# Feed-forward units with the hi and lo halves of the input side by side, and the linear operand's row factor moved to the norm behind

## The reference

```python
def conv_gated_ffn(h, w_in, conv_w, conv_b, w_out):      # D_FF = 2816
    g, u = jnp.split(h @ w_in, 2, axis=-1)
    gp = jnp.pad(g, ((0, 0), (CONV_WIDTH - 1, 0), (0, 0)))
    g = conv_b + sum(conv_w[k] * gp[:, k:k + S] for k in range(CONV_WIDTH))
    return (jax.nn.gelu(g) * u) @ w_out

# twice, i = 0, 1
h = conv_gated_ffn(rms_norm(x, norm_ffn_pre[i]), ffn_w_in[i], ffn_conv_w[i], ffn_conv_b[i], ffn_w_out[i])
x = x + rms_norm(h, norm_ffn_post[i])
```

## Time and profile before

| | us |
|---|---|
| median of 3 runs | 1108.94 (1108.13 to 1110.29) |
| profiled execution, its own time | 1108.64 |
| its span | 1106.5 |
| TensorE busy | 1074.8 |
| VectorE busy | 781.8 |
| ScalarE busy | 642.5 |
| GpSimd busy | 96.8 |

### The profile page before, as it was taken

How to read it: one execution, slowest core, us unless ns; L and a number is a source line. 1 busy time by engine, 2 the same in 40 slices (tenths; PEclk the granted TensorE clock), 3 DMA queues, 4 the chain that set the end, 5 groups by cost and what they waited for, 6 DMA issues and landing times.

```text
span 1106.5 us, 20061 instructions
## 1 busy us (share of the span) xinstructions
PE 1074.8 (97%) x6870; PEld 949.7 (86%) x6870; DVE 781.8 (71%) x1331; ACT 642.5 (58%) x1158; POOL 96.8 (9%) x119
## 2 busy tenths in 40 slices
PE   8989999999999999999999999999999998999998
PEld 7967999999788998777999999899678887888886
DVE  6657877777654367886877777698779748666664
ACT  6658444444764855666444444677777747554443
POOL 0140111111010002220111111000100000000000
PEclk9999999999999999999999999999999999999999
DMA  9353665555366475442665555265212544555541
GB/s 340 103 197 113 224 195 184 197 190 191 114 247 199 125 228 171 153 152 77 213 203 190 189 192 190 77 221 180 96 39 71 175 155 154 190 188 190 190 152 38
DMA packets 51380, 185.06 MB, mean 167 GB/s; under 512 B 5728, under 2 KB 6240, under 8 KB 51328
## 3 DMA queue, kind: packets, MB, share of 16 engines
q1 hardware_dynamic: 49248, 178.28, 48.4%
q0 software_dynamic: 1504, 5.44, 1.4%
q10 hardware_dynamic: 576, 0.64, 0.2%
HBM read 183.29 MB, written 1.05 MB: 167 GB/s over the span
## 4 chain that ended last, share of the span: by engine, by line
PE 86%; DVE 8%; ACT 3%; issue 2%; DMA 0%; DVEq 0%; SPq 0%; ACTq 0%
PE ps L228 28%; PE ps L173 15%; PE ps L175 15%; PE ps L174 15%; PE ps L198 5%; DVE w_lo L156 3%; PE ps L200 2%; PE ps L1612 1%; ACT both L430 1%; DVE arena L815 1%; DVE both L436 1%; PE ps L750 1%; PE ps L734 1%; PE ps L721 1%; PE ps L1623 1%
## 5 line engine op out<-in xcount | busy, mean ns | idle before, releaser
L156 DVE TENSOR_TENSOR w_lo<-raw,w_hi 128x1024 fp32r<-128x1024 f32 x336 | 418.0, 1254 | 118.5 <-ACT w_hi L151 116.7
L151 ACT ACTIVATE w_hi<-raw 128x1024 fp32r<-128x1024 f32 x336 | 346.9, 1052 | 98.8 <-PE ps L175 51.3
L173 PE MATMUL ps<-both,w_hi 128*128 128x256 f32 x1152 | 328.0, 285 | 1.9 <-DVE both L436 0.9
L174 PE MATMUL ps<-both,w_hi 128*128 128x256 f32 x1152 | 326.2, 283 | 0.0
L175 PE MATMUL ps<-both,w_lo 128*128 128x256 f32 x1152 | 326.2, 283 | 0.0
L228 PE MATMUL ps<-w_hi,both 128*128 128x512 f32 x992 | 293.8, 396 | 7.3 <-DVE both L1197 3.3
L173 PEld LDWEIGHTS ps<-both,w_hi 128*128 128x128 f32 x1152 | 221.1, 192 | 6.2 <-issue 2.9
L174 PEld LDWEIGHTS ps<-both,w_hi 128*128 128x128 f32 x1152 | 221.2, 192 | 1.5
L175 PEld LDWEIGHTS ps<-both,w_lo 128*128 128x128 f32 x1152 | 221.1, 192 | 0.0
L228 PEld LDWEIGHTS ps<-w_hi,both 128*128 128x128 f32 x992 | 178.8, 188 | 45.6 <-DVE w_lo L156 4.3
L228 PE MATMUL ps<-w_lo,both 128*128 128x512 f32 x496 | 158.2, 392 | 0.0
(11 more groups left out here) (199 smaller groups left out, 1095.8 us busy)
## 6 DMA issues: line engine op xcount, KB each, us to landing
raw<-in_w SPq DMA_DIRECT2D x336, 512.0 KB, 3.4
row<-in_rows POOLq DMA_DIRECT2D x7, 512.0 KB, 4.2
x<-in_x SPq DMA_DIRECT2D x2, 512.0 KB, 4.4
out<-x SPq DMA_DIRECT2D x4, 256.0 KB, 2.1
misc<-in_misc POOLq DMA_DIRECT2D x1, 512.0 KB, 5.7
arena<-in_ws POOLq DMA_DIRECT2D x1, 512.0 KB, 7.7
tab<-in_tables POOLq DMA_DIRECT2D x1, 320.0 KB, 4.4
tab<-in_tables POOLq DMA_DIRECT2D x1, 256.0 KB, 4.6
```

What stands on the lines that cost most here:

```text
L151: act.activation(w_hi[:, s, :], raw[:, s, :], ACT.Copy).then_inc(hi_done, 1)
L156: dve.tensor_tensor(w_lo[:, s, :], raw[:, s, :], w_hi[:, s, :].bitcast(F32), ALU.subtract).then_inc(lo_done, 1)
L173: pe.matmul(o, l_hi, r_hi, start=first, stop=False)
L174: pe.matmul(o, l_hi, r_lo, start=False, stop=False)
```

## The change

Gate and linear units of both gated feed-forwards go through `features_apart`. ScalarE copies the second half of each bank to SBUF (`F_GP`, `F_UP`), and VectorE adds the two halves (`F_GS`, `F_US`). The gate is still multiplied by `ROW`, after the sum. The product is now gelu times the summed linear operand, without the factor; GpSimd has no part in it. TensorE waits for `f.summed` of t-2 where it waited for `f.product` of t-2. On VectorE the sum of the linear unit and the product come ahead of `split(1)`. Updates 1 and 3 get power 1, and `factors_dve` saves their factors ahead of the feed-forward.

```diff
-    F_CV, F_GL, F_PR, F_GR = cut(3072, 2, SEQ), cut(3584, 2, SEQ), cut(4096, 2, SEQ), cut(4608, 2, SEQ)
+    F_CV, F_GL, F_PR = cut(3072, 2, SEQ), cut(3584, 2, SEQ), cut(4096, 2, SEQ)
+    F_UP, F_US, F_GP, F_GS = (cut(4608 + 512 * k, 2, SEQ) for k in range(4))
...
     def ffn_in_pe(pe, f, n0, t, i=0):
         if t >= 3:
-            pe.wait_ge(f.product, t - 1 + 2 * i)
+            pe.wait_ge(f.summed, t - 1 + 2 * i)
         g_bank, u_bank = f_banks(t, i)
-        features(pe, f_g(n0, t), ps[:, g_bank, 0:SEQ], i)
-        features(pe, f_g(n0, t) + 1, ps[:, u_bank, 0:SEQ], i)
+        features_apart(pe, f_g(n0, t), g_bank, i)
+        features_apart(pe, f_g(n0, t) + 1, u_bank, i)
...
     def ffn_pe(pe, f, n0, u, following, turn_early=True):
-        features(pe, n0, ps[:, 0, 0:SEQ], pre=after(u))
+        features_apart(pe, n0, 0, pre=after(u))
         row_pe(pe, u, 1)
-        features(pe, n0 + 1, ps[:, 3, 0:SEQ])
+        features_apart(pe, n0 + 1, 3)
...
     def ffn_act_step(act, f, n0, t, i, split):
         b = t % 2
+        act.wait_ge(unit_used, f_g(n0, t) + 1 + RING * i)
+        if t >= 2:
+            act.wait_ge(f.gate_summed, t - 1 + 2 * i)
+        act.activation(F_GP[:, b, :], ps[:, f_banks(t, i)[0], SEQ:2 * SEQ], ACT.Copy).then_inc(f.gate_part, 1)
         split(0)
         act.wait_ge(f.conv, 3 * t + 3 + 6 * i)
         if t >= 2:
-            act.wait_ge(f.scaled, t - 1 + 2 * i)
+            act.wait_ge(f.product, t - 1 + 2 * i)
         act.activation(F_GL[:, b, :], F_CV[:, b, :], ACT.Gelu_apprx_tanh).then_inc(f.gelu, 1)
+        act.wait_ge(unit_used, f_g(n0, t) + 2 + RING * i)
+        if t >= 2:
+            act.wait_ge(f.summed, t - 1 + 2 * i)
+        act.activation(F_UP[:, b, :], ps[:, f_banks(t, i)[1], SEQ:2 * SEQ], ACT.Copy).then_inc(f.part, 1)
         split(1)
...
-    def ffn_pool_step(pool, f, t, i=0):
-        b = t % 2
-        pool.wait_ge(f.gelu, t + 1 + 2 * i)
-        if t >= 2:
-            pool.wait_ge(f.product, t - 1 + 2 * i)
-        pool.tensor_tensor(F_GR[:, b, :], F_GL[:, b, :], ROW, ALU.mult).then_inc(f.scaled, 1)
...
     def ffn_dve_step(dve, f, n0, layer, t, i, split):
...
-        dve.wait_ge(unit_used, f_g(n0, t) + 1 + RING * i)
-        dve.tensor_tensor(pad[:, b, 2:2 + SEQ], ps[:, g_bank, 0:SEQ], ROW, ALU.mult).then_inc(f.copied, 1)
+        dve.wait_ge(f.gate_part, t + 1 + 2 * i)
+        dve.tensor_tensor(F_GS[:, b, :], ps[:, g_bank, 0:SEQ], F_GP[:, b, :], ALU.add).then_inc(f.gate_summed, 1)
+        dve.wait_ge(f.gate_summed, t + 1 + 2 * i)
+        dve.tensor_tensor(pad[:, b, 2:2 + SEQ], F_GS[:, b, :], ROW, ALU.mult).then_inc(f.copied, 1)
...
         split(0)
+        dve.wait_ge(f.part, t + 1 + 2 * i)
+        dve.tensor_tensor(F_US[:, b, :], F_UP[:, b, :], ps[:, u_bank, 0:SEQ], ALU.add).then_inc(f.summed, 1)
+        dve.wait_ge(f.gelu, t + 1 + 2 * i)
+        dve.wait_ge(f.summed, t + 1 + 2 * i)
+        dve.tensor_tensor(F_PR[:, b, :], F_GL[:, b, :], F_US[:, b, :], ALU.mult).then_inc(f.product, 1)
         split(1)
-        dve.wait_ge(f.scaled, t + 1 + 2 * i)
-        dve.wait_ge(unit_used, f_g(n0, t) + 2 + RING * i)
-        dve.tensor_tensor(F_PR[:, b, :], F_GR[:, b, :], ps[:, u_bank, 0:SEQ],
-                          ALU.mult).then_inc(f.product, 1)
         dve.wait_ge(f.hi, t + 1 + 2 * i)
...
-               for n, (begins, power) in enumerate(((N_FFN0, 0), (N_SGV, 0), (N_FFN1, 0), (N_MIX, 0), (N_MLP, 0), (UNITS, 2)))]
+               for n, (begins, power) in enumerate(((N_FFN0, 0), (N_SGV, 1), (N_FFN1, 0), (N_MIX, 1), (N_MLP, 0), (UNITS, 2)))]
...
             dve.wait_ge(pad_ready, 2)
+            factors_dve(dve, updates[1])
             ffn_dve(dve, ffn[0], N_FFN0, 0)
             update_dve(dve, updates[1], 2, 2, True)
             sgu_dve(dve)
             update_dve(dve, updates[2], 3, 3, False, 3)
+            factors_dve(dve, updates[3])
             ffn_dve(dve, ffn[1], N_FFN1, 1)
```

More of the change, by code:

```diff
@@ L529, in last_update_dve @@
             add_dve(dve, u, tt)
-    F_CV, F_GL, F_PR, F_GR = cut(3072, 2, SEQ), cut(3584, 2, SEQ), cut(4096, 2, SEQ), cut(4608, 2, SEQ)
+    F_CV, F_GL, F_PR = cut(3072, 2, SEQ), cut(3584, 2, SEQ), cut(4096, 2, SEQ)
+    F_UP, F_US, F_GP, F_GS = (cut(4608 + 512 * k, 2, SEQ) for k in range(4))
     def ffn_sems(name):
-        return signals(name, "copied conv gelu scaled product hi lo")
+        return signals(name, "gate_part gate_summed copied conv gelu part summed product hi lo")
     def f_g(n0, t):
@@ L592, in ffn_act_step @@
         split(2)
-    def ffn_pool_step(pool, f, t, i=0):
-        b = t % 2
-        pool.wait_ge(f.gelu, t + 1 + 2 * i)
-        if t >= 2:
-            pool.wait_ge(f.product, t - 1 + 2 * i)
-        pool.tensor_tensor(F_GR[:, b, :], F_GL[:, b, :], ROW, ALU.mult).then_inc(f.scaled, 1)
-    def ffn_pool(pool, f):
-        pool.wait_ge(next_sems.row_out, f_row[f])
-        for t in range(2):
-            ffn_pool_step(pool, f, t)
-        with pool.Fori(0, (FT - 2) // 2) as i:
-            for t in (2, 3):
-                ffn_pool_step(pool, f, t, i)
     def ffn_dve_step(dve, f, n0, layer, t, i, split):
@@ L2149, in _ @@
             load_row(3)
-            ffn_pool(pool, ffn[0])
             updated(1)
@@ L2155, in _ @@
             load_row(5)
-            ffn_pool(pool, ffn[1])
             updated(3)
```

## The result

The changed kernel takes **1104.48 us** (median of 6 runs, 1102.6 to 1105.77), the kernel before 1109.7 in the runs beside it (6 runs, 1108.13 to 1110.29). The ratio is 0.995, with a 95% interval of 0.9939 to 0.996: 5.2 us or 0.5% faster, where 3.7 us had been forecast. The profiled execution took 1104.57 us with a span of 1102.8; that of before has a span of 1106.5.

The account below looks back on a forecast made before the run. TensorE, busy 97%, was taken as the bound: -4.2 us from its matmuls, +0.2 start, +0.2 end and +0.1 updates make -3.7, so 1105.2 us. The range was 1101.5 to 1108.2, the forecast's own about 1103.5 to 1106.7.

Parts of the forecast that it names:

- TensorE is the bound, and the gain is its own: Gated feed-forwards: with fewer matmuls a TensorE block takes 8.405 us against 8.50, 4.2 us less over 44 blocks.
- This 13 ns beyond the columns is what a dropped matmul can give: TensorE's short matmul costs 0.120 us against 0.107 for 256 columns; the difference was called what dropping one can save.
- large gain: Rival: TensorE's gated units take 2.78 us and nothing is given back, total about 1101 us; chance 0.12.
- small gain: Rival: little saved per dropped matmul, seams give some back; 1106.8 to 1108.5 us, mostly within 0.2%; chance 0.16.
- VectorE's step: Gated loops: two adds more but waits gone, 7.89 us instead of 8.25, so VectorE catches up with TensorE's 8.40.
- Start: Start of each gated feed-forward: TensorE waits before g(3) for VectorE's linear sum of t = 1; 0.1 us each.
- End: Last held units of each gated feed-forward: `a_lo` done 4.0 to 4.6 us behind TensorE's last unit; 0.1 us lost each.
- Updates: Updates 1 and 3: `term_dve` with a factor takes 746 ns against 684; 0.06 us lost each, 0.12 in all.
- VectorE becomes the bound: Rival: waits stay in the gated loops, VectorE's step 9.17 us, deciding from 8.7 on; about 1120 us; chance 0.07.

Follow-up runs that it names:

- Experiment 1: Changed kernel with the 512-column matmul as two of 256 in seven of eight contraction blocks: 1108.06 us, ratio 0.9984 to the kernel before.
- experiment 2: Kernel before with only the factor moved to the norm, no GpSimd multiplication, three short matmuls kept: 1109.21 us, ratio 0.9995.
- experiment 3: Changed kernel with GpSimd's multiplication by the factor back and no factor power at the updates: 1103.55 us, ratio 0.995.
- experiments 9 and 10: Changed kernel with each unit's long and short matmuls grouped, in gated and plain feed-forwards: by eights 1098.85 us, by twos 1097.96 us.
- Experiments 6 to 8: Changed kernel, `w_lo` matmuls split into two of 128 columns: 1174.52 us; Experiment 1, two of three matmuls mostly halved: 1098.42; changed kernel, short matmul mostly halved: 1098.01.
- experiment 4: Changed kernel with VectorE's second `w_lo` ahead of the linear sum and product again: 1161.99 us, ratio 1.0464.
- experiment 5: Changed kernel with one, two or three scratch 256-column additions in each VectorE step of the gated feed-forwards: 1104.72, 1107.24 and 1126.46 us.

## Why the prediction was right, and where not

- **TensorE is the bound, and the gain is its own: right.** Experiment 1 takes most of it back (3.8 of 4.7 us) with nothing else touched; experiments 2 and 3 show the factor's move as neutral, as the prediction costed it. The unit of the plain feed-forward was the right twin: 2.81 and 2.83 us were forecast and measured. The term was mis-sized only in the accumulation behind it, 2.74 to 2.75 us instead of 2.765. Both bodies together gave 4.7 us, their start losses included, for 4.2 - 0.2 = 4.0.
- **"This 13 ns beyond the columns is what a dropped matmul can give": wrong in this form.** 4.7 us over 704 matmuls are 6.7 ns each. The sum didn't use the sentence, but it misled on where the rest lay: dropping 13 ns a piece would have made the unit 2.77. The other half is what the alternating stream takes beyond its matmuls in groups, and experiments 9 and 10 get most of it back. The Trainium skill's fixed 2.5 ns for a warm matmul ("TensorE: Matmul & The Clock Gate", "Wait — 56ns, not 53.3ns?") would have given 1107.6, an estimate, and is not borne out by this stream, whose matmuls of 512 and 256 columns take 13 to 15 ns beyond their columns. The section "Back-to-back issue gap" of the Trainium skill's same page says that in a stream of weight load and matmul pairs the spacing is set by both, with about 81 ns at 128 columns and 131 ns at 512. Experiments 6 to 8 agree with the first part, but they measured 113 and 228 ns, and that decides here.
- **The rivals "large gain" and "small gain" did not happen.** The units take 2.81 and 2.83 us, not 2.78, and the ratio's upper bound of 0.996 leaves out 1106.8 to 1108.5. But the large gain's unit of 2.78 is real. It is what the same instructions take in pairs, and in some profiles also in the old order, at the start of the plain feed-forward. To set it aside for the loop's rows came out right in the gated feed-forwards; that one order has two paces, the prediction did not know.
- **VectorE's step: mechanism right, 0.3 us too long.** 7.89 forecast, 7.57 measured. The terms that failed are the seams of `w_lo`: 1.14 from the first one's start to the next operation's (156.37 to 157.51) instead of 1.22, the same behind the other two (158.36 to 159.50, 159.96 to 161.11), 0.34 from the product to `w_lo` (158.02 to 158.36) instead of 0.49; the convolution was right to 0.02. It catches up and is then paced by the gate's copy, as forecast. That this needs the new order, experiment 4 shows: 9.27 us and 57 us lost.
- **Start: mechanism wrong, size right by luck.** There is no wait for the sum at g(3): the sum of t = 1 is done at 122.61 and TensorE comes to g(3) at 123.67. VectorE's step is 5.75 us there (113.02 to 118.77), not 6.0 to 6.8, and its sum is done 3.84 behind the step's start, not 4.15; the prediction took 1.59 from the loop for the convolution, which is 1.37 here (113.94 to 115.31). TensorE waits 0.21 us at 109.48 for `w_lo` instead, and not at all in the second feed-forward. That this is together the 0.2 of the sum is chance.
- **End: forecast 0.1 for each, measured 0** (9.60 and 9.59). `a_lo` is done 3.74 us behind the last unit, not 4.0 to 4.6, since the step is 0.3 shorter; 4.1 was right as what TensorE allows, as experiment 5 shows.
- **Updates: right.** 0.06 forecast for each, 0.07 measured for update 1 and 0.06 for update 3, and the group by line has the duration used (beside the earlier trace rows), now with eight half tiles more:

```profile
L451 DVE SCALAR_TENSOR_TENSOR arena<-ps,st,row 128x512 f32<-128x512 f32 x12 | 8.7, 745 | 12.1 <-issue 6.4 <-ACT arena L407 4.5 <-PE ps L228 1.3
```

- **The rival "VectorE becomes the bound": its chance stood, its formula was wrong.** "A lag of 9 allowed", deciding "from a step of 8.7 us on", counts only the wait inside the loop. The lag must be gone before the last two steps: with 3 us of it at the loop's entry a step of 8.39 - 3 / 16 = 8.2 in the loop is the limit, not 8.7, and less if the steps around the loop grow too: 1.2 us for each feed-forward at 8.06, 22 us in all at 8.40. Additions in the last steps cost even under that limit: 0.9 us in all with one of them. The price of 15 us for a step of 9.17 was too small by the same mistake: at 9.3 it is 39 us of waits, and 57 with the clock.
- **The total:** 5.2 us for 3.7. 0.9 of the difference is TensorE's, the starts' and the ends' (-4.7 + 0.14 instead of -3.7). The other 0.6 is not settled: between update 1 and the second feed-forward the changed kernel is 0.6 us shorter (292.67 to 518.26 against 293.55 to 519.74), though nothing is changed there. Every other profile has 225.5 to 225.7 us in this stretch, and the one of the kernel before alone has 226.2; experiment 2 with its matmuls and experiment 3 with its factor have 225.6 too. So neither part of the change makes this difference. Experiment 1 keeps some 1 us that its long matmuls don't explain, and the interval of the ratio is 1.2 us to either side. It may be no effect at all.

## What to carry to other kernels

Where one engine's stream is the bound and its instruction has a twin elsewhere in the same trace, take the twin's price in the same surroundings, seams included, and don't argue from what "must" be overhead. Ask of a second engine in a pipelined loop not only whether its step is shorter than the period, but whether (period - step) x steps pays back the lag with which it enters, before the stage drains. And once a loop mixes two sizes of matmul, try them in pairs: here it was worth about as much as the change itself.

## What was not expected of the hardware

- With a weight load for each, a 128-column fp32r matmul takes 0.113 us from start to start, a 256-column one 0.120, a 512-column one 0.228. Below 256 columns almost nothing is saved (experiments 6 to 8).
- A stream that alternates 512- and 256-column matmuls has two paces, 0.347 and 0.353 us for the two. Both show at the start of the plain feed-forward, in different profiles of the same instructions; in the loops it is 0.351 to 0.354. In groups of two or eight the loops run at 0.346 to 0.350, which is worth 6.5 us of 1104 here.
- A wait of TensorE can cost more than its length: in the windows at waits of 3.88 and 4.56 us in experiments 5 and 4 the granted clock was 0.74 and 0.51, and the lower clock took some 7 and 16 us of the whole time. The length of the wait alone does not decide: with three additions a wait of 2.25 us in the first feed-forward was followed by 0.52 (282 to 284 us), one of 2.24 in the second by 0.94 (707 to 709). It was also 0.93 over 25 us of the changed kernel's profile with the same work that ran at 1.00 before.
- Two VectorE additions of 256 columns that don't need each other take 0.335 us from start to start, while the gate's sum and the multiplication that needs it are 0.46 apart (153.54 to 154.00).
